# A hybrid decoder layer with an order planned by hand: gates on ScalarE, fewer top-k sums, a hand-over through DRAM, and two new rules of order

## The reference, cut to what matters

```python
v1, i1 = lax.top_k(s1, 16);  v2, i2 = lax.top_k(s2, 16)
cand = (v1[..., :, None] + v2[..., None, :]).reshape(..., 256)
sv, si = lax.top_k(cand, 16)
eid = take(i1 * 128 + i2, si);  gate = softmax(sv)
hval = einsum('thkd,td->thk', u_emb[eid], xb)
y = einsum('thk,thkd->td', gate * gelu(hval), v_emb[eid])
```

## Time and profile before

| what | value |
|---|---|
| median of 3 runs | 3857.44 us (3857.39 to 3862.43) |
| the profiled execution's own time | 3870.04 us |
| its span, first to last instruction | 3868.2 us |
| instructions | 31404 |
| busy share PE / DVE / ACT / POOL | 82% / 69% / 26% / 32% |
| mean granted TensorE clock | 0.93 of full speed |

### The profile page before, as it was taken

One profiled execution on the slowest core, in us unless ns is written; L12 is line 12 of the kernel. 1 busy time (PEld: TensorE's weight loads), 2 busy tenths in 40 slices (PEclk: granted clock), 3 DMA queues, 4 the chain that ended last, 5 costly groups with the idle time before them and its releaser, 6 DMA issues.

```text
span 3868.2 us, 31404 instructions
## 1 busy us (share of the span) xinstructions
PE 3178.7 (82%) x9551; PEld 1543.8 (40%) x9551; DVE 2674.1 (69%) x6543; ACT 993.7 (26%) x2512; POOL 1237.8 (32%) x1084
## 2 busy tenths in 40 slices
PE   5999864988798879887987898689887389879776
PEld 2444253443354325433543453245433144334321
DVE  1222138888868778978888888988856998434655
ACT  1111122152134214421432153115222022311211
POOL 0000001444444434443443344234342124333443
PEclk9999977999999999998999899899999699889999
DMA  4111133999999999999999999889998179988998
GB/s 170 57 66 50 54 116 134 391 417 397 392 404 407 415 370 369 394 399 361 397 400 368 364 385 408 341 341 384 356 394 340 70 297 420 392 338 343 414 421 341
DMA packets 190425, 1245.72 MB, mean 322 GB/s; under 512 B 22704, under 2 KB 27184, under 8 KB 50672
## 3 DMA queue, kind: packets, MB, share of 16 engines
q0 software_dynamic: 155520, 1128.34, 72.4%
q1 hardware_dynamic: 34736, 115.37, 7.9%
HBM read 1220.50 MB, written 22.46 MB: 321 GB/s over the span
## 4 chain that ended last, share of the span: by engine, by line
PE 44%; DMA 26%; DVE 24%; issue 3%; ACT 1%; SPq 1%; POOL 1%; DVEq 0%; ACTq 0%; POOLq 0%
PE yacc L1030 23%; DMA weights<-in_uv,eid 19%; PE bank L857 11%; DVE weights L1484 7%; DVE kv L1346 3%; DVE tiny L1345 3%; PE bank L993 3%; DMA weights<-in_w_out 2%; PE bank L967 2%; DVE weights L1416 1%; DVE weights L1215 1%; DVE weights L1412 1%; DMA kv<-in_cache_ik,gi 1%; POOL weights L1838 1%; ACT diag L1747 1%
## 5 line engine op out<-in xcount | busy, mean ns | idle before, releaser
L1030 PE MATMUL yacc<-weights,diag 128*128 128x512 f32 (+1 forms) x4224 | 2002.5, 624 | 364.7 <-ACT diag L1747 363.4
L1838 POOL DMA_INDIRECT weights<-in_uv,eid x1056 | 1210.5, 1146 | 2578.1 <-PE yacc L1030 1875.8
L1484 DVE CUSTOM_DVE_ANT_0 weights<-weights,xn 128x1024 f32<-128x1024 f32 x1056 | 1290.2, 1224 | 597.5 <-DMA weights<-in_uv,eid 585.8
L1030 PEld LDWEIGHTS yacc<-weights,diag 128*128 128x128 f32 (+1 forms) x4224 | 802.5, 196 | 1453.6 <-issue 909.3
L1747 ACT ACTIVATE diag<-main,coef 128x128 f32<-128x128 f32 x1024 | 356.7, 394 | 1450.8 <-DVE coef L1475 1381.1
L1345 DVE MAX8 tiny<-kv 128x8 f32<-128x384 f32 (+6 forms) x224 | 245.0, 1094 | 3.0
L1755 ACT ACTIVATE gl<-hv 128x2 f32<-128x2 f32 x528 | 107.1, 203 | 530.6 <-DVE hv L1484 529.9
L1346 DVE MATCH_REPLACE8 kv<-tiny,kv 128x384 f32<-128x384 f32 (+6 forms) x224 | 241.6, 1079 | 0.0
L967 PE MATMUL bank<-weights 128*128 128x512 f32 (+1 forms) x288 | 158.4, 687 | 87.0 <-DMA weights<-in_w_out 85.8
L857 PE MATMUL bank<-weights 128*128 128x512 f32 (+3 forms) x560 | 229.6, 572 | 0.0
L857 PE MATMUL bank<-weights,mid 128*128 128x512 f32 (+1 forms) x448 | 183.2, 570 | 0.0
(11 more groups left out here) (240 smaller groups left out, 2309.8 us busy)
## 6 DMA issues: line engine op xcount, KB each, us to landing
weights<-in_w_out SPq DMA_DIRECT2D x72, 512.0 KB, 7.8
weights<-in_uv,eid POOLq DMA_INDIRECT x1056, 9.8
Hb<-h_scratch SPq DMA_DIRECT2D x8, 1700.0 KB, 10.7
weights<-in_w_in SPq DMA_DIRECT2D x6, 2048.0 KB, 18.8
h_scratch<-Hb SPq DMA_DIRECT2D x4, 1700.0 KB, 5.5
h_scratch<-spare SPq DMA_DIRECT2D x4, 1700.0 KB, 5.5
nw<-in_wffn SPq DMA_DIRECT2D x9, 512.0 KB, 6.4
nw<-in_wfin SPq DMA_DIRECT2D x9, 512.0 KB, 14.3
```

The costliest lines, as they stand in the source:

```text
L1030: mm = nc.tensor.matmul(yacc[0:W, 512 * j:512 * (j + 1)], diag[:, n % 4, 0:W], ring[:, n % RING, D + 512 * j:D + 512 * (j + 1)], start=Fal ...
L1484: ins = V.tensor_tensor_reduce(u, u, xn[:, t % 2, :], 1.0, 0.0, ALU.mult, ALU.add, hv[:, n % RING:n % RING + 1])
L1838: pool.indirect_dma_start(dst, None, table, bass.IndirectOffsetOnAxis(ap=ids, axis=0)).then_inc(s, 16)
```

## The change

- `weigh_pair` on DVE goes. ACT's `unit(t, k)` now does gelu, two products by the gate (a Copy with the gate as scale, one column each) and the two diagonals, with waits on its own results between them. The `drain` entries go.
- `cand` keeps 136 of 256 sums per head: row 0 with all 16 columns, and rows 1 to 15 with the first 8. `pick` gets three small instructions to undo the new numbering.
- The front ends with `stash`: SP writes both halves of the mix from `Hb` to DRAM (`m_scratch`). The next `load` waits for that in place of `mixT`. The back begins with `remix`, which reads it into `h1`; `mixT` transposes from there, and `resid` loads the residual over it once `mixT` has run.
- Retention becomes a stream of its own (`side_steps`) beside the front, and the first 24 `slogits` steps of the sample one more (`past_steps`).
- POOL gathers the rows at a `fetch` entry of their own, listed as soon as the sums that free the buffers are listed. The cache gathers stay at the entries of PE's steps.
- In the planner a unit and its sums are due before everything but `seed` and `finish`; sums count as ready 2.0 us after the dots; `PERIOD` 400 becomes 360, `LEAD` 150 becomes 100, `NEAR` 0.4 becomes 0.1.

```diff
+CAND = PK + (PK - 1) * PK // 2
...
-    return steps + [Step("mixT", t, 0, "P", 2.6, 1, 2.4)]
+    return steps + [Step("stash", t, 0, "", 0, 1, 5.0)]
...
-    steps = [Step("resid", t, 0, "", 0, 0, 4.0)]
+    steps = [Step("remix", t, 0, "", 0, 0, 4.0), Step("mixT", t, 0, "P", 2.6, 1, 2.4), Step("resid", t, 0, "", 0, 0, 4.0)]
...
-PERIOD, LEAD, ROW, LATENCY, NEAR = 400.0, 150.0, 2.62, 3.4, 0.4
+PERIOD, LEAD, LATER, LAST, ROW, LATENCY, NEAR = 360.0, 100.0, 0.0, 1.2, 2.62, 3.4, 0.1
...
-                yield "D", at, t * PERIOD + PERIOD * k / units(0), "unit"
+        if dot in fetched:
+            yield "D", fetched[dot], -1e7, "unit"
+        if fetch[0] <= TILES and arrival(*fetch) is not None:
+            yield "", 0.0, 0.0, "fetch"
...
-            yield "P", weighed[t, k] + 1.0, t * PERIOD + PERIOD * k / units(0), "sums"
+            yield "P", weighed[t, k], -1e7, "sums"
+        if copying and (copying[0][0] == TILES or copying[0][0] + 1 in keyed):
+            yield "", copying[0][1], 0.0, "ycopy"
...
+                elif what == "stash":
+                    sp.wait_ge(mix_ready, t + 1)
+                    sp.wait_ge(gated, t + 1)
+                    if t == SAMPLE:
+                        sp.wait_ge(att_in, 16 * NB * KVH)
+                    sp.dma_start(m_dram[t * P:t * P + R, 0:512], Hb[0:R, 0:512]).then_inc(mix_out, 16)
+                    sp.dma_start(m_dram[t * P:t * P + R, 512:D], Hb[0:R, GR:GR + 512]).then_inc(mix_out, 16)
+                elif what == "remix":
+                    if t:
+                        sp.wait_ge(seeded, t)
+                    sp.wait_ge(mix_out, 32 * (t + 1))
+                    sp.dma_start(h1[0:R, :], m_dram[t * P:t * P + R, :]).then_inc(mix_in, 16)
...
-                    if k and s == PAIR * k:
-                        weigh_pair(t, k - 1)
...
+                act.wait_ge(hval_ready, n0 // PAIR + 1)
+                A.activation(gl[:, c:c + PAIR], hv[:, c:c + PAIR], ACT.Gelu).then_inc(gelu_ready, 1)
+                act.wait_ge(gelu_ready, n0 // PAIR + 1)
+                for s in range(PAIR):
+                    ins = A.activation(coef[:, c + s:c + s + 1], gl[:, c + s:c + s + 1], ACT.Copy,
+                                       scale=gates[:, PAIR * k + s:PAIR * k + s + 1])
+                ins.then_inc(coef_ready, 1)
...
-            def unit(t, k):
+            def fetch(t, k):
```

More of the change, by code:

```diff
@@ L268, in front_steps @@
         steps += [Step("splace", t, 0, "D", 9.0, 1, 0.3)]
[L269 to L272, removed]
+        steps += [Step("topk", t, k, "D", 4.8, 0, 0.3) for k in range(ROUNDS)]
         steps += [Step("mask", t, 0, "D", 1.4, 0, 0.3)]
@@ L356, in make_schedule @@
     clock = {"P": 0.0, "D": 0.0}
-    fronts = [Stream(front_steps(t), (t - 2) * PERIOD - LEAD, PERIOD) for t in range(TILES + 1)]
+    fronts = [Stream(front_steps(t), (t - 2) * PERIOD - LEAD + (t == SAMPLE) * LATER, PERIOD if t < TILES else LAST * PERIOD)
+              for t in range(TILES + 1)]
     backs = [Stream(back_steps(t), (t - 1) * PERIOD, 0.9 * PERIOD) for t in range(TILES + 1)]
-    front = back = 0
+    sides = [Stream(side_steps(t), (t - 2) * PERIOD - LEAD, 0.5 * PERIOD) for t in range(TILES + 1)]
+    pasts = [Stream(past_steps(), (SAMPLE - 2) * PERIOD + LATER, PERIOD)]
+    front = side = back = past = 0
     rows_at = 0.0
     chosen, keyed, mixed, seeded, finished, kept = {}, {}, {}, {}, {}, {}
-    dotted, weighed, summed = {}, {}, {}
-    dot, pair, drained = (0, 0), (0, 0), 0
+    turned, held, returned, placed = {}, {}, [], []
+    weighed, summed, copying = {}, {}, []
+    dot, pair, fetch, fetched = (0, 0), (0, 0), (0, 0), {}
     def arrival(t, k):
+        if t not in chosen:
+            return None
         free = chosen[t] + LATENCY
@@ L386, in candidates @@
                 continue
+            if what in ("decay", "sdecay"):
+                ready = max(ready, turned[t])
+            if what == "stash" or (what, part) in (("attend", 3), ("sscores", 0)):
+                if t not in held:
+                    continue
+                ready = max(ready, held[t])
+            if what == "sturn":
+                if not returned:
+                    continue
+                ready = max(ready, returned[0])
+            if what == "slogits" and part == (0, 0):
+                ready = max(ready, held[t], placed[0])
+            if what == "smask" and part == (0, 0):
+                if not past:
+                    continue
+                ready = max(ready, pasts[0].ends[-1])
             if what == "mixT" and t:
@@ L424, in make_schedule @@
             start = max(clock[on], start)
-        if kind in ("front", "back"):
-            stream = fronts[front] if kind == "front" else backs[back]
+        if kind in ("front", "side", "back", "past"):
+            stream = {"front": fronts[front:], "side": sides[side:], "back": backs[back:], "past": pasts}[kind][0]
             e = stream.head()
@@ L437, in make_schedule @@
                 keyed[t] = end
-            if what == "mixT":
+            if what == "stash":
                 mixed[t] = end
+            if (what, part) in (("turn", 3), ("spad", 0)):
+                turned[t] = end
+            if what == "sret":
+                returned.append(end)
+            if what == "splace":
+                placed.append(end)
+            if what == "retained" and part == 2:
+                held[t] = end
             if stream.head() is None and kind == "front":
                 front += 1
+            elif stream.head() is None and kind == "side":
+                side += 1
+            elif stream.head() is None and kind == "past":
+                past += 1
             elif stream.head() is None:
@@ L1882, in svalue @@
                 gather(gathered_v[bb % 2], table_v, gi[:, 4 * g + bb:4 * g + bb + 1], g_in[bb % 2])
-            steps = {"unit": unit, "sscores": sscores, "slogits": slogits, "svalue": svalue}
+            steps = {"fetch": fetch, "sscores": sscores, "slogits": slogits, "svalue": svalue}
             for what, t, part in schedule:
```

140 lines of the change are left out of this document (69 added, 71 removed).

## The result

The changed kernel takes 4082.99 us (median of 4 runs, 4080.53 to 4085.66) beside 3859.93 for the kernel before (3857.39 to 3866.78) on the same chip: a ratio of 1.0575, interval 1.0557 to 1.0593. It is slower by 222 us. I had forecast 3765 us and faster; both the sign and the range (3620 to 3890) were wrong.

The account below looks back on a forecast made before the run. The prediction took DMA row gathers as the bound, gaining only where they stop. Its terms, -80 - 25 - 45 + 15 + 5 + 38 = -92 us, from 3857.44 gave 3765 us; own range 3700 to 3835, wider range 3620 to 3890.

Parts of the forecast that it names:

- The gathers' places, +38: At 24 cache gathers, now issued level with PE: PE waits each landing, partly covered by the ring; +38 us.
- upper bound that I had written: For the 24 cache gathers: 24 x 8.6 = +206 us if the ring of rows in flight covers nothing.
- the first rival: Cache gathers stop the row stream at PE's 24 steps: 206 in place of 38, 3933 us; chance 0.20.
- the ring's cover of 10 us: Row gathers in flight keep DMA busy some 10 us of a PE stop, 12 with 2 us won by gates.
- Dots first, -80 - 25 - 45: Dots due ahead of topk: idle DMA returns at 2990 to 3090, in neighbouring windows, and at tile boundaries.
- The third term: At four tile boundaries: -45 of 71 us idle DMA returns, bounds 0 and -71.
- The first two terms: Sample's topk stretch: -80 at 2990 to 3090, -25 at 3090 to 3190 and 2940 to 2990.
- the third rival: Dots first make fronts, backs and `chosen` late; the boundary loses what the tile won; about 3855 us, chance 0.07.
- the second rival: Stream runs full, fronts ahead of rows: 3692 us, or 3590 if the rate rises towards 422 GB/s; chance 0.28.
- 136 sums: Fewer candidate sums save 44 us of DVE: nothing in the stream, 5 us at tile 0.
- The hand-over, +15 and +5: Mix through DRAM: +15 us for 8.6 MB of traffic, +5 for tile 0 waiting on both trips.
- The signs that I had named "wrong": 24 cache waits with sample's-stretch DMA at 0.7 or less; `mixT` waits over 10 us; POOL awaiting gates after tile 0.

Follow-up runs that it names:

- E9: Kernel before, with only POOL's row gathers moved right behind the sums that free their buffers, rows kept in order: 4053.34 us, ratio 1.0490.
- E2: Changed kernel with POOL's row gathers written at the place of their dots again: 3882.67 us, ratio 1.0045.
- E6: Kernel before with dots and sums due first in the list's planner: 3916.08 us, ratio 1.0130.
- E7: Kernel before with only the gate products moved to ACT: 3853.93 us, ratio 0.9966.
- E8: Kernel before with only 136 in place of 256 candidate sums per head: 3859.19 us, ratio 0.9981.
- E12: Kernel before with dots and sums first, gates on ACT and 136 sums together: 3883.53 us, ratio 1.0047.
- E11: Changed kernel with 13 of the 24 cache gathers written two units earlier in POOL's order: 3957.81 us, ratio 1.0235.
- E13: Changed kernel with row gathers at their dots' place and 16 of the sample's 32 topk rounds left out: 3803.81 us, ratio 0.9844.
- E10: Changed kernel with row gathers at their dots' place, dots and sums due over their tile, other planner numbers: 3826.95 us, ratio 0.9899.

## Why the prediction was wrong

Taken alone, the parts come to +189 (E9; 205 by E2) + 50 (E6) - 13 (E7) - 7 (E8) = +219 to +235 us. With the three small ones measured together (E12, +18) it is +207 to +223. The hand-over is near 0 (E2 against E12). Measured: +222. My sum was -92.

- **The gathers' places, +38: the step that failed most.** It measured 189 to 205 us, near the upper bound that I had written (206, if the ring covers nothing). The mechanism was the first rival's, word for word: the gather is the last thing in the queue, and DMA is dry when PE resumes. I took the ring's cover of 10 us from the stop at `out`, where the late transfer was not in the rows' queue and not behind them. Here the landing of the gather is itself the sign that the ring is empty, so PE's step, the sums and POOL's issue (10 us in the trace above) have no cover; the step alone took 4.75 us where I had 3. Over 24 gathers this is 205 / 24 = 8.5 us, against 5.4 from which the rival decided. But only 17 of them stopped PE, so a real stop cost about 12 us (10 by E11). The 8.6 us of my bound has no working in the prediction; that it came so near is in part luck. The rival's chance of 0.20 was too low by the row that spoke for it. The rule of the Trainium skill, page "DMA: Bandwidth & Descriptors", section Rules for kernel authors (issue a DMA early, wait on it late), is what this part of the change broke. E11 agrees: two units of earlier issue return 10 us for each gather moved.
- **Dots first, -80 - 25 - 45: the second step that failed.** Alone it measured +50. The third term looks right in its place: the four boundaries of the earlier trace rows lost 71 - 22 = 49 us of idle time. But the boundary of tile 6, which the term did not count, took back 39 of them, with POOL waiting 42.6 us for its gates. E6 had nothing of the term: from the first row of tile 0 to the first of tile 6 its DMA share is 0.96, as before (0.97 in the changed kernel). The first two terms were wrong: I let the displaced topk rounds "fill DVE's waits for rows". They could not. They start only when all scores of the sample are in, 27 to 44 us after the last gather of index keys lands in the kernel before, the changed one and E6. Before, that landing comes 59 us into tile 6, in E6 288 us and in the changed kernel 404 us, and the rounds then find 12 and 5 of its 64 units still to come; most of them stand between two tiles, ahead of the back of tile 7 (E6, E13). This is the third rival, to which I gave 0.07: fronts and backs late, `chosen` late, and what was won inside the tile lost at the boundary. Two rivals came true at once, and I had priced each alone.
- **The rate.** I argued that full windows at different rates are no sign of a shallow queue. From 690 to 2740 us 26 of 41 windows of 50 us run at 420 to 422 GB/s in the changed kernel, 4 in the kernel before. E12 reaches 397 of the mean of 407 with three parts; the rest came with the hand-over or its planner numbers (argued from the difference, not tried alone). E2, without the rows' own place, has 407 too. So the second rival's rise was half there: from 385 / 0.96 = 401 to 407 / 0.99 = 411 while busy. DMA share in this stage: forecast 0.97 to 0.98, measured 0.99.
- **Gates on ACT.** Gelu is followed at once by the two copies, as forecast, in 0.72 us from gelu's start to the second copy's end, against 2.97 before (1413.54 to 1416.51). The copies last longer than the 203 ns that I took:

```profile
L1799 ACT ACTIVATE gl<-hv 128x2 f32<-128x2 f32 x528 | 106.8, 202 | 1388.9 <-DVE hv L1542 1388.3
...
L1802 ACT ACTIVATE coef<-gl,gate 128x1 f32<-128x1 f32 x1056 | 253.3, 287 | 17.3
```

  253 us on ACT in place of 214, which costs nothing at 30% busy. In the kernel before this part was worth -13 us; I gave it nothing.
- **136 sums.** A FIND_INDEX8 over 136 columns takes 294 ns in the changed kernel, where I had said close to 284. Forecast -5 as a part of tile 0, measured -7.
- **The hand-over, +15 and +5.** PE does stand at `mixT`: 127.7 us in nine waits, as I had said of the store and the landing. The wait at the start of tile 1, with the store of `y` just ahead of the load (columns as above; SPq is SP's queue):

```profile
1008.09 0.34 SPq L749 DMA_DIRECT2D out_y_p<-nw  x1
...
1008.53 0.38 SPq L853 DMA_DIRECT2D h<-m_scratch  x1
...
1020.03 1.57 PEld L1015 LDWEIGHTS bank<-main,h 128*128 128x128 f32 x8 [14.09 <-DMA h<-m_scratch]
```

  The ring covers most of it: DMA is at 0.85 in the 50 us around this stop, and the four boundary windows above, each with such a stop inside, are at 0.94 to 0.99. Tile 0 did not lose 5 us, its first row went out 7 us earlier (E12, without the hand-over, starts at 650.0, as before). Why, I have not tried.

The signs that I had named "wrong" all came: waits at the cache with DMA at 0.58 to 0.79 in the sample's stretch, waits at `mixT` of over 10 us (seven of the nine), and POOL waiting for gates after tile 0. The first and third carried the loss, the second did not. One sum of the chances does not close: 0.20 and half of 0.07 are 0.235, not the 0.21 given for slower.

Open: the hand-over was not tried alone in the kernel before, so its share in the rate and in the 37 us between E12 and the changed kernel at tile 6 is only a difference. Whether a lighter topk for the sample, with the full choice, would return the rest of E10's slow stretch was not tried either.

## What to carry to other kernels

Where one queue carries a stream and single transfers, look at what is in flight when the single one lands. Here it was issued last, so its landing meant an empty queue, and the price of the stop was the whole way back to the first new byte (10 us in the stop shown), not the wait that the profile shows. Giving one kind of work the first rank in a list does not make the other kind vanish: ask when the displaced work becomes ready and what is left beside it by then. When a change moves the events, move the windows with them before you compare: the windows of the earlier trace rows, left in their old places, would show 6.5 us of idle time at the boundaries where there are 22, and none of the 40 at tile 6. And when two rivals rest on different mechanisms, they can both come true; price them together.

## What the runs showed that I had not expected

- In a stop of PE of 12 us the granted clock fell from 1.00 to 0.50 (1.2 of 2.4 GHz; the 2 us windows above), and PE's step after it ran at 0.50 to 0.58: the eight transposes took 1.97 us, against 1.09 in E2 where PE came straight from sums. So a stop also lengthens the step that ends it.
- A one-column copy on ACT, with its scale read from a tile, took longer than gelu on two columns: mean 287 ns against 202.
- Row gathers landed later (median 11.7 us after issue, before 9.8) while the stream moved more: 407 GB/s against 385.
